# A one-core hybrid decoder layer (sparse attention, Mamba-2, gated DeltaNet, MLP) in fp32: two projection blocks joined, convolution and gates in one block, a fused state update, a reordered start of the MLP block

## The reference

```python
h = rmsnorm(x, g_mix)
qa, ka, va, qi, ki, wi, zb, xbc, dtb, qkv, zc, a_raw, b_raw = split_proj(h @ w_in_l)   # 2048 x 7784
q = rmsnorm(qa.reshape(Bsz, T, H_A, DH_A), qn) * ATTN_SCALE
k = rmsnorm(ka.reshape(Bsz, T, H_A, DH_A), kn)
o_a = attn_fn(q, k, v, qi, ki, wi)        # top-k over the cache of 4096 keys (sample) or over the prompt
...
xbc, new_buf = causal_conv_silu(xbc_raw, conv_buf, conv_w, conv_b)       # 4 taps along time, both mixers
dt = jax.nn.softplus((dt_raw + dt_bias).astype(jnp.float32))
S_new = Sf * jnp.exp(cum[:, -1])[:, :, None, None] + jnp.einsum('bshn,bshp->bhpn', bc * w_end, xdt)
...
q = l2norm(q.reshape(Bsz, T, H_C, DK_C)) * (DK_C ** -0.5)
g = -jnp.exp(A_log.astype(jnp.float32)) * jax.nn.softplus((a_raw + dt_bias).astype(jnp.float32))
beta = jax.nn.sigmoid(b_raw)
S_new = Sf * jnp.exp(last)[..., None] + jnp.einsum('bhjk,bhjv->bhkv', kc * jnp.exp(last - cum)[..., None], u)
...
mix = jnp.concatenate([o_a.reshape(Bsz, T, D_A), o_b, o_c], axis=-1)
x = x + mix @ w_out_l
hm = rmsnorm(x, g_mlp)
x = x + jnp.square(jax.nn.relu(hm @ w_up_l)) @ w_down_l                  # 2048 x 8192 x 2048
```

## Time and profile before

| what | value |
|---|---|
| time, median of 3 runs (lowest, highest) | 3632.32 us (3630.06, 3635.02) |
| the profiled execution: its time, its span | 3625.24 us, 3623.4 us |
| PE, DVE, ACT, POOL busy | 3210.1, 2186.9, 564.8, 1419.0 us |
| mean granted TensorE clock | 0.934 |
| DMA moved | 360.30 MB, 99 GB/s |

### The profile page before, as it was taken

How to read it: one execution, slowest core, us unless ns; L and a number is a source line. 1 busy time by engine, 2 the same in 40 slices (tenths; PEclk the granted TensorE clock), 3 DMA queues, 4 the chain that set the end, 5 groups by cost and what they waited for, 6 DMA issues and landing times. The chain is left out here.

```text
span 3623.4 us, 54272 instructions
## 1 busy us (share of the span) xinstructions
PE 3210.1 (89%) x22287; PEld 2955.0 (82%) x22287; DVE 2186.9 (60%) x3229; ACT 564.8 (16%) x1074; POOL 1419.0 (39%) x853
## 2 busy tenths in 40 slices
PE   7978997999993477783997999999999999999998
PEld 6935886899772377752886999999999999999998
DVE  7025994898318666446896755546555555555554
ACT  3222211122325211114321200000000000000000
POOL 4353332476323232313333444434444343444442
PEclk9989998999995698776998999999999999999999
DMA  5322332478643000217333222322323222222232
GB/s 181 95 78 83 107 88 77 128 218 253 204 143 102 17 1 1 54 51 206 96 99 135 67 91 83 94 83 85 91 82 94 82 91 83 87 85 89 83 94 97
DMA packets 415941, 360.30 MB, mean 99 GB/s; under 512 B 26362, under 2 KB 367962, under 8 KB 414309
## 3 DMA queue, kind: packets, MB, share of 16 engines
q1 hardware_dynamic: 379664, 287.06, 27.0%
q0 software_dynamic: 13440, 42.02, 3.6%
q10 hardware_dynamic: 22592, 27.59, 2.3%
HBM read 311.63 MB, written 46.20 MB: 99 GB/s over the span
## 5 line engine op out<-in xcount | busy, mean ns | idle before, releaser
L3067 POOL TENSOR_TENSOR om_ring<-om_raw,om_mask 128x1024 fp32r<-128x1024 f32 x264 | 680.7, 2579 | 937.2 <-DVE om_ring L3185 937.2
L3107 PE MATMUL om_ps<-om_h,om_ring 128*128 128x272 f32 x6144 | 780.3, 290 | 21.6 <-issue 18.1
L3107 PEld LDWEIGHTS om_ps<-om_h,om_ring 128*128 128x128 f32 x6144 | 777.6, 190 | 24.1 <-issue 23.9
L3107 PE MATMUL om_ps<-om_hid,om_ring 128*128 128x272 f32 x6144 | 770.6, 288 | 0.0
L3107 PEld LDWEIGHTS om_ps<-om_hid,om_ring 128*128 128x128 f32 x6144 | 769.8, 188 | 0.0
L3185 DVE CAST om_ring<-om_mask 128x1024 fp32r<-128x1024 f32 x264 | 455.2, 1724 | 9.1
L321 POOL TENSOR_TENSOR w_ring<-w_raw,w_mask 128x1024 fp32r<-128x1024 f32 (+2 forms) x110 | 259.5, 2378 | 370.5 <-DVE w_mask L452 210.3
L372 PE MATMUL pm_ps<-h,w_ring 128*128 128x280 f32 x2688 | 363.7, 297 | 26.2 <-issue 11.5
L372 PEld LDWEIGHTS pm_ps<-h,w_ring 128*128 128x128 f32 x2688 | 356.0, 193 | 33.7 <-issue 26.6
L3193 DVE TENSOR_TENSOR om_x<-om_x,om_ps 128x272 f32<-128x272 f32 x288 | 112.7, 433 | 357.8 <-PE om_ps L3107 354.5
L390 PE MATMUL pq_ps<-w_ring,h 128*128 128x512 f32 (+2 forms) x1440 | 291.3, 364 | 7.7 <-POOL w_ring L321 7.6
(11 more groups left out here) (521 smaller groups left out, 3668.9 us busy)
## 6 DMA issues: line engine op xcount, KB each, us to landing
om_raw<-in_w_up SPq DMA_DIRECT2D x128, 512.0 KB, 4.1
om_raw<-in_w_down SPq DMA_DIRECT2D x128, 512.0 KB, 3.6
w_raw<-in_w_in SPq DMA_DIRECT2D x112, 512.0 KB, 3.8
ao_raw<-in_w_out SPq DMA_DIRECT2D x32, 384.0 KB, 4.0
as_qb<-q_rows SPq DMA_DIRECT2D x32, 256.0 KB
projT<-pm_stage ACTq DMA_DIRECT2D x56, 140.0 KB
conv_x<-projT SPq DMA_DIRECT2D x28, 280.0 KB, 2.7
xT_scratch<-ln_xT SPq DMA_DIRECT2D x1, 4480.0 KB, 15.4
```

The lines of the kernel that those rows point to most:

```text
L3067: pool.tensor_tensor(f32r(ring[:, s, 1, half_of(q)]), raw[:, q, :], mask[:, q, :], ALU.subtract).then_inc(split[q], 1)
L3107: ins = pe.matmul(ps[bank][:, 0:HM], w, f32r(src[:, b, k, kept_half(half)]), start=first, stop=last)
```

## The change

1. The blocks "pq", `sample_inputs` and "pm" become one `project_in` over plan[3:], loads 0 to 23 of kind N and 24 to 51 of kind F. `ChooseThenAttend` runs the new `Choose`, which holds the instructions of `sample_inputs` at fixed places, and then `AttendSample` 24 loads later. PSUM now holds the banks of both, so that token tiles rotate over 5 banks (4 and the attention's `dead_bank`) and not 8.
2. The instructions of `gates` go into `convolve` at passes AT_GATES = 4 to 12 and AT_SQUARES = 24 to 29, and the copies `big_copy` move from DVE to ACT (`tokens_out`).
3. Each state update is 4 `scalar_tensor_tensor` of 128 columns in place of two `tensor_tensor` of 512.
4. The attention block no longer waits until its last 4 stores to `mixT` have landed; the last block asks SP for weights first and waits before it reads `mixT`. In its first chunk DVE masks both halves, makes the low part of half 0 itself and casts after that; POOL makes only the low part of half 1.

```diff
@@ project_in @@
+        feature_out = min((first_out[n] for n in range(N) if loads[n].kind == "F"), default=0) if side else 0
+        token_ps = ps + (side.token_banks if side else [])
+        def bank_of(b):
+            return token_ps[b % len(token_ps)] if side and b < feature_out else ps[(b - feature_out) % banks]
+        def bank_free(pe, b):
+            if side and b < feature_out:
+                if b >= len(token_ps):
+                    pe.wait_ge(evac, b - len(token_ps) + 1)
+            elif b - feature_out >= banks:
+                pe.wait_ge(evac, b - banks + 1)
+            elif feature_out:
+                pe.wait_ge(evac, feature_out)
@@ convolve, ACT @@
+            def tokens_out(f):
+                n = nth[f]
+                act.wait_ge(turned, n + 1)
+                act.activation(sb["tm"][:, 0:4, n * P:(n + 1) * P], big[n % 2][:, :, :], ACT.Copy)
+                act.activation(sb["tm"][0:TAIL, 4, n * P:(n + 1) * P], small[n % 2][0:TAIL, :], ACT.Copy
                                ).then_inc(small_out, 1)
+            def gate_steps(f):
+                if f == AT_GATES + 1:
+                    act.wait_ge(g_par_in, 128)
+                    act.activation(rate[:, :], alog[:, :], ACT.Exp).then_inc(rate_ready, 1)
+                    act.wait_ge(za, 1)
+                    act.activation(u[:, :, :], w[:, :, :], ACT.Exp, scale=-1.0).then_inc(exp_u, 1)
+                    act.activation(beta[:, :, :], raw[:, :, 18:24], ACT.Exp, scale=-1.0).then_inc(exp_b, 1)
+                if f == AT_GATES + 3:
+                    act.wait_ge(wr, 1)
+                    act.activation(lw[:, :, :], w[:, :, :], ACT.Ln).then_inc(ln_w, 1)
+                if f == AT_GATES + 8:
+                    act.wait_ge(done, 1)
...
+                i = f - AT_SQUARES
+                if 0 <= i < 5:
+                    act.wait_ge(small_out, nth[F_Q + 2 * HC - 1] + 1)
+                    if i:
+                        act.wait_ge(summed, i)
+                    act.activation(squares[0:n, :, :], ..., ACT.Square).then_inc(sq_ready, 1)
@@ scans_tail, DVE (both halves alike) @@
-                    now = s_nat[:, 4 * half:4 * half + 4, q, :]
-                    s_step(dve.tensor_tensor(now, now, bc(el_nat[:, q, 4 * half:4 * half + 4].unsqueeze(2), [P, 4, NB]),
-                                             ALU.mult))
                     dve.wait_ge(s["upd"], x + 1)
-                    dve.tensor_tensor(now, now, e_ps[x % 2][:, :, :], ALU.add).then_inc(s["upd_out"], 1)
+                    for j in range(4):
+                        b = 4 * half + j
+                        now = s_nat[:, b, q, :]
+                        last = dve.scalar_tensor_tensor(out=now, in0=now, scalar=el_nat[:, q, b:b + 1],
+                                                        in1=e_ps[x % 2][:, j, :], op0=ALU.mult, op1=ALU.add)
+                    last.then_inc(s["upd_out"], 1)
@@ class Choose @@
+    def sync(self, sp, n, stored):
+        if n == 16:
+            sp.wait_ge(stored[0], 32)
...
+            sp.dma_start(sb["s_qkv"][:, :], dram["projN"][TP:TOK, 0:3 * DA]).then_inc(s["in"], 16)
...
+        if n == 23:
+            sp.wait_ge(s["normed"], 1)
+            sp.dma_start(dram["q_rows"], sb["s_qkv"][:, 0:DA]).then_inc(s["saved"], 16)
@@ attend_and_project, output_and_mlp @@
-                sp.dma_start(dram["mixT"][:, TOK * h:TOK * h + TP], outT[:, h, :]).then_inc(s["mix_saved"], 16)
-            sp.wait_ge(s["mix_saved"], 16 * HA)
+                sp.dma_start(dram["mixT"][:, TOK * h:TOK * h + TP], outT[:, h, :]).then_inc(sb["mix_saved"], 16)
...
             x_t = dram["xT"].rearrange("p (k t) -> p k t", k=KT)
+            sp.wait_ge(sb["mix_saved"], 16 * HA)
...
-            lows(0, 0)
+            pool.wait_ge(masked_w[1], 1)
+            pool.tensor_tensor(f32r(ring[:, 0, 1, half_of(1)]), raw[:, 1, :], mask[:, 1, :], ALU.subtract).then_inc(split[1], 1)
@@ build @@
-            project_in(nc, dram, sb, plan[3:9], "pq", BANKS, side=Choose(nc, sb))
-            sample_inputs(nc, dram, sb)
-            project_in(nc, dram, sb, plan[9:], "pm", 4, side=AttendSample(nc, dram, consts, sb))
+            project_in(nc, dram, sb, plan[3:], "pm", 4, side=ChooseThenAttend(nc, dram, consts, sb))
```

More of the change, by code:

```diff
@@ L431, in _ @@
                         act.wait_ge(stored[b % 4], 16 * (b // 4))
-                    act.activation(stage[rows, b % 4, 0:cols], ps[b % banks][rows, 0:cols], ACT.Copy).then_inc(evac, 1)
+                    act.activation(stage[rows, b % 4, 0:cols], bank_of(b)[rows, 0:cols], ACT.Copy).then_inc(evac, 1)
                     act.wait_ge(evac, b + 1)
@@ L538, in convolve @@
         dest = lambda f: sb["bcT"][:, f - F_B, :] if F_B <= f < F_Q else feat[:, f % R, :]
+        raw, bias, alog = sbuf("g_raw", [P, 5, 24]), sbuf("g_bias", [P, 18]), sbuf("g_alog", [P, 18])
+        z, u, w, lw, t = (sbuf(f"g_{n}", [P, 5, 18]) for n in "z u w lw t".split())
+        rate = sbuf("g_rate", [P, 18])
+        by_block = sbuf("g_by_block", [P, 9, 18])
+        squares, rn = sbuf("g_squares", [P, 2 * HC, P]), sb["rn"]
+        ps = ctx.enter_context(nc.psum_tensor("g_ps", [P, 5, 36], F32))
+        pe_ps = ctx.enter_context(nc.psum_tensor("g_el", [P, 13, 18], F32))
+        g_par_in, cleared, raw_in, g_chain, exp_u, ln_w, exp_b, rate_ready, g_ready, sums, cums, done = (
+            sem(f"g_{n}") for n in ("par_in", "cleared", "raw_in", "chain", "exp_u", "ln_w", "exp_b", "rate_ready",
+                                    "g_ready", "sums", "cums", "done"))
+        za, wr, sq_ready, summed, root = (sem(f"g_{n}") for n in ("za", "wr", "sq_ready", "summed", "root"))
+        g, dt, beta = sb["g"], sb["dt"], sb["beta"]
         block = ctx.enter_context(nc.Block())
@@ L559, in _ @@
         def _(pool):
+            pool.memset(raw[:, :, :], 0.0).then_inc(cleared, 1)
             for n in range(R):
@@ L1565, in delta @@
                     h, half = divmod(x, 2)
-                    now = st_smp[:, 4 * half:4 * half + 4, h, :]
-                    decay = sb["el"][:, 5 + 4 * half:9 + 4 * half, 12 + h:13 + h]
-                    d_step(dve.tensor_tensor(now, now, bc(decay, [P, 4, P]), ALU.mult))
                     dve.wait_ge(d["upd"], x + 1)
-                    dve.tensor_tensor(now, now, a_ps[x % 2][:, :, :], ALU.add).then_inc(d["upd_out"], 1)
+                    for j in range(4):
+                        b = 4 * half + j
+                        now = st_smp[:, b, h, :]
+                        last = dve.scalar_tensor_tensor(out=now, in0=now, scalar=sb["el"][:, 5 + b, 12 + h:13 + h],
+                                                        in1=a_ps[x % 2][:, j, :], op0=ALU.mult, op1=ALU.add)
+                    last.then_inc(d["upd_out"], 1)
                 yield
@@ new lines, with __init__, sync, tensor @@
+class ChooseThenAttend:
+    def __init__(self, nc, dram, consts, sb):
+        self.choose, self.attend = Choose(nc, dram, sb), AttendSample(nc, dram, consts, sb)
+        self.dve_lows = TOKEN_LOADS + DVE_LOWS
+    def enter(self, ctx):
+        self.attend.enter(ctx)
+        self.choose.enter(ctx, self.attend)
+        self.token_banks = [self.attend.dead_bank]
+    def sync(self, sp, n):
+        if n < TOKEN_LOADS:
+            self.choose.sync(sp, n, self.stored)
+        else:
+            if n == TOKEN_LOADS:
+                sp.wait_ge(self.choose.s["saved"], 48)
+            self.attend.sync(sp, n - TOKEN_LOADS)
+    def tensor(self, pe, place):
+        if place < 2 * TOKEN_LOADS:
+            self.choose.tensor(pe, place)
+        else:
+            if place == 2 * TOKEN_LOADS:
+                pe.wait_ge(self.choose.s["out"], 1)
+            self.attend.tensor(pe, place - 2 * TOKEN_LOADS)
+    def scalar(self, act, place):
+        if place < 2 * TOKEN_LOADS:
+            self.choose.scalar(act, place)
+        else:
+            self.attend.scalar(act, place - 2 * TOKEN_LOADS)
+    def gpsimd(self, pool):
+        return self.attend.gpsimd(pool)
+    def pool_steps(self, n):
+        return self.attend.pool_steps(n - TOKEN_LOADS) if n > TOKEN_LOADS else 0
+    def vector(self, dve):
+        spent = 0
+        for share in self.choose.vector(dve):
+            spent += share
+            yield share
+        yield SHARE * TOKEN_LOADS - spent
+        dve.wait_ge(self.choose.s["saved"], 48)
+        for share in self.attend.vector(dve):
+            yield share
@@ L3258, in gain @@
                 mask_tile(KA + k, gained_tile(k))
-            highs(0, 0, None)
+            for q in range(PARTS):
+                dve.wait_ge(raw_in[q], 16)
+                dve.tensor_scalar(bits(mask[:, q, :]), bits(raw[:, q, :]), HIGH, None, ALU.bitwise_and).then_inc(masked_w[q], 1)
+            dve.wait_ge(masked_w[0], 1)
+            dve.tensor_tensor(f32r(ring[:, 0, 1, half_of(0)]), raw[:, 0, :], mask[:, 0, :], ALU.subtract).then_inc(split[0], 1)
+            for q in range(PARTS):
+                dve.wait_ge(masked_w[q], 1)
```

(1 more changed line is left out.)

371 lines of the change are left out of this document (163 added, 208 removed).

## The result

| | before | after |
|---|---|---|
| time, median of 4 runs (lowest, highest) | 3631.19 us (3629.33, 3635.02) | 3574.47 us (3572.04, 3581.62) |
| the profiled execution: its time, its span | 3625.24, 3623.4 us | 3581.62, 3579.8 us |
| ratio, 95% interval | | 0.9845 (0.9833 to 0.9857) |

The change takes 56.7 us (52 to 61 by the ratio's interval, 1.43 to 1.67% of 3631). The profiled execution of before (3625.24) was quicker than all four runs of its row, and that of after was the slowest of its four, so the two traces are only 43.6 us apart. In the traces 10.8 of it stand in stretches whose code did not change: the scans are 5.3 longer, the way from them to the first state update 3.7, the gap ahead of the convolution's taps 1.1, the attention 0.7.

A forecast was written before the change was run, and what follows sets the result against it. PE was taken as the bound, computing 3210 of 3623 us. 30 + 21 + 7 + 2.5 = 60.5 off the profiled 3625.24 gave 3565; the median, 0.2% above, gave 3572, range 3556 to 3597.

The forecast's parts named there:

- The join: Token to feature loads: sample inputs move inside the projections, DVE starts attention 27.7 earlier; value 30 us, bounds 20 and 31.
- the rival with that pace: Sample attention keeps PE's pace, so the join yields 20 and the whole change 50 us (3582); chance 0.14.
- the 2.3 that I added for waits that shrink: At the join: 2.3 us extra because PE's and DVE's waits for each other in the attention would shrink together.
- The copies: Convolution: 24 DVE passes each lose a 0.60 us copy to ACT, 14.4 us, with DVE still setting the pace.
- The rival of an ACT-paced pass: Convolution: ACT sets the pace, at 2.8 us a pass; the part yields about 10 to 13 us (3583); chance 0.14.
- Gates and squares before the last tap: Convolution: gate steps 7.0, table switches 3.1 and squares 9.4 us are added ahead of the last tap.
- the detours: Convolution: three ACT passes load another function table and the old one again; 3.1 us left over on the path.
- The squares: Convolution from pass 25: reduce, square and SiLU alternate with the taps, making the passes 9.4 us longer in sum.
- Behind the last tap: From last tap to the scans' first product: 38 us shrink to about 12, so 26 less.
- The update: State updates in the tail: four fused operations, 1.1 us in all, give a 1.25 period; value 7, bounds 9 and 1.
- The last block: Start of the last block: weights come some 3 us earlier, x tiles 2.2; value 2.5, bounds 1 and 3.5.
- Slower, or given back: Five token banks make PE wait at chunk starts (3644, chance 0.03), or POOL's gathers set attention's end (3632, chance 0.03).

The follow-up runs named there:

- experiment 1: Kernel before with only the joined projection block (sample inputs inside): 3592.47 us against 3617.21, ratio 0.9930.
- experiments 7 and 8: Changed kernel with DVE delayed by three further match_replace (3567.53 us), and with PE delayed by 80 further small transposes (3562.11 us).
- experiment 6: Kernel before with the token tile copies moved from DVE to ACT, gates still in their own block: 3609.07 us against 3618.08, ratio 0.9977.
- experiment 12: Changed kernel with the gates' exponentials and logarithm replaced by scaled copies, so no table loads in the convolution: 3563.27 us, ratio to before 0.9847.
- experiment 11: Changed kernel with two buffers for the squares in place of one: 3556.34 us, ratio to the kernel before 0.9823.
- experiments 10: Changed kernel with the state update of before put back: 3567.49 us, ratio to the kernel before 0.9848.

## Why the prediction was right

The forecast was 3572 and the measured 3574.5; the gain of 60.5 was 56.7, and 55.9 in the second session. Added up from the stages the parts give 25.7 (join), 23.3 (convolution and gates), 4.8 (update) and 3.0 (last block), 56.8 in all. Part of the closeness is luck: the join was put 4 to 5 too high and the update 2 too high, and the convolution 2 too low. Point by point:

- **The join, 30 predicted, 24.7 measured.** The mechanism was right, above all that DVE's start counts and not PE's: PE's start moved 19.5, and the rival with that pace (20) is refuted by the traces, where the end of the features moved by 25.7; experiment 1's 24.7 and the traces of experiments 7 and 8 agree. The mis-sized term is the last one, the 2.3 that I added for waits that shrink. PE's wait for `as_hit` did shrink from 6.26 to 3.2, but it is PE's, and DVE, which sets the end, still waits 5.6 for PE. The shift of DVE's start itself was 25.5 and not 27.7: the second mask was done at 613.8 and not at 611.8, since the split of the first feature load began 1.2 later than I put it (603.27 to 602.1), and its halves were split by 605.67 and 608.70 in place of 604.6 and 607.1, the moments at which the next raw halves can be asked for. For the second half it waited for the mask of 603.55, which took 2.68 beside POOL's first half in place of 0.69.
- **The copies, 14.4 predicted, 13.8 measured** (experiment 6). ACT's copy took 0.577, as the row of another block said (0.59), and DVE kept the pace: ACT waited for it in 24 passes, 13.8 us, or 0.58 a pass, more than the 0.25 that I had left it. The rival of an ACT-paced pass is refuted. In the changed kernel ACT still waits in 16 passes (9.4 us); in the others stand the detours and the squares, where DVE waits for ACT's first tap.
- **Gates and squares before the last tap, 19.5 predicted, 18.1 measured** (92.6 - 74.5). Within it the detours were put at 3.1 and are worth 1.4 (experiment 12). The rule of the Trainium skill's page "ScalarE: Activation LUTs", section "What ACT_TABLE_LOAD costs", of 1.38 us of drain at each table switch, would have made that 8.3 more by an estimate from the page's figure. The trace does not agree: the first exponential begins 0.02 us behind the load's end, and the six loads in the convolution begin 0.02 to 0.08 behind the activation ahead of them. Experiment 12 by itself could not tell, because of the 7.7 us that six loads take (6 x 1.28) only 1.4 reached the taps. The squares were taken as 9.4, and experiment 11 shows of what they are made: 5.0 of it is not work but the ring through the one buffer.
- **Behind the last tap, 26 predicted, 27.7 measured**, so the two stages together gave 23.3 against 21.
- **The update, 7 predicted; 4.4 in its stage, 4.8 with the shorter last operation.** From the first update's start to the last one's the first half gave 1.7 (15.4 to 13.7; 1.65 predicted) and the second 5.0 (19.1 to 14.1; 5.3 predicted), where L1568's stretching went. The mean period is 1.25 and 1.28, as I took it: the first two intervals of a half are 1.6 to 1.7, those from the fourth update on 1.17 and 1.20. The terms that I left out take 1.9 back: from the last update of the first half to the first of the second it is 6.8 us, 5.4 before, and the very last update takes 1.12 in place of 0.69. Whether it shows in the time is not settled: alone it gave -0.6 (interval of the ratio 0.9990 to 1.0008), undone in the changed kernel 5.8. From the first addition or fused operation to the end of the last one it is 40.4 to 40.8 in the seven profiles with the old update and 34.5 to 35.8 in the seven with the new, so the stage's own gain is clear of noise.
- **The last block, 2.5 predicted, 2.4 measured alone**, at the limit of what the runs tell. The traces bear it out: from the last product of the attention's projection to the first of the last block it is 20.0 to 20.8 us in the eight profiles with part 4 and 22.5 to 23.4 in the six without, and "rest" is 1921.8 in the mean of the eight and 1925.2 in that of the six.
- **Slower, or given back**: from the first token product to the first feature product it is now 293.0, with 0.7 of transposes and 0.8 of wait in it, and from the first to the end of the last token product it was 291.4 before (318.1 to 609.5), so five banks made nothing wait.

The single parts sum to 46.0 us by medians and the whole is 55.9. The intervals of the four ratios together are about 0.24% wide to each side, 9 us, and that of the whole 0.14%; so the gap of 10 is at the edge of what they tell (by the ratios it is 13, beyond it), and its cause stays open. Part 2 and part 3 are the ones whose single runs gave less than their stages did (19.4 for 23.3, and -0.6 for 4.8). What the stage table offers is that stages with the same code vary: the scans 172.9 to 180.1, and the rest 1916.9 to 1924.8 where part 4 is in it. In the scans the high values are frequent where part 2 or one of its halves is present (seven of ten profiles at 179 or more, none of the four without), but experiments 10, 11 and 12 have it and took 172.9 to 174.9. What the length does go with is the granted clock in the scans: its mean is 0.90 in the four profiles at 174.7 to 174.9, 0.88 in the two at 177.8 and 177.9, 0.85 in the seven from 179.2 to 180.1, and 0.91 in the one at 172.9. Whether part 2 makes the lower clock more frequent, and so gives back some 3 us there, is open.

## What to carry to other kernels

Where two engines are nearly equally loaded, find out whose start moves with the edit, and count that shift, not the idle time seen on the other; a delay put in on each of them in turn, read in the trace and not only in the time, shows which one it is. When work is slipped into a paced loop, look for the ring that it closes through its buffers (here reduce, square, first tap, taps) before counting it as work: a second buffer gave back 8 us of stage time. An edit of under 5 us should be judged by its stage in several profiles, since unchanged stages moved by as much, together with their granted clock.

## What the runs showed of the hardware

- The same code of the scans took 172.9 to 180.1 us in fourteen profiles, and its length went with the mean granted clock in it: 0.91 at 172.9, 0.90 at 174.7 to 174.9, 0.88 at 177.8 and 177.9, 0.85 at 179.2 to 180.1. In windows of 10 us the clock lay between 0.50 and 1.00; the engine had been at 0.50 (1.2 GHz) through the convolution and up to the scans, before and after the change.
- Four `scalar_tensor_tensor` of 128 columns, with a column as scalar and PSUM as second input, took 1.12 us together, 0.28 each, although a single one's record is 0.34; none was stretched beside POOL's products, where the `tensor_tensor` with both inputs in SBUF went from 0.69 to 1.81.
- A function table's load took 1.28 us, and the next activation began 0.02 us behind it; six of them fewer shortened a stretch of 92.8 us by 1.4.
